# Attention's phases in the order outputs, corrections, scores, transposes, in place of scores, corrections, outputs, transposes

## The reference

```python
# q: 16 heads of 64; k, v: 2 heads of 64; blocks of 128 tokens; window of 128
kb = concat([previous block of k, this block], axis=2)     # vb the same
s = einsum('bnqkgd,bnskd->bnkgqs', q, kb) * HEAD_DIM ** -0.5
band = (sj <= qi + BLOCK) & (sj > qi + BLOCK - WINDOW)     # 128 keys per query
s = where(mask, s, -inf)
probs = softmax(concat([s, sink]))[..., :-1]
o = einsum('bnkgqs,bnskd->bnqkgd', probs, vb)
yb = (o * silu(a_gate)) @ w_br_attn
```

## Time and profile before

| | us |
|---|---|
| median of three runs | 1083.79 |
| the profiled execution | 1083.33 |
| its span | 1081.4 |
| PE busy | 1076.3 |
| DVE busy | 859.7 |
| ACT busy | 494.5 |
| POOL busy | 378.3 |
| scores of round 4 to scores of round 15 | 549.56 to 648.60 |

### The profile page before, as it was taken

How to read it: one execution, slowest core, us unless ns; L and a number is a source line. 1 busy time by engine, 2 the same in 40 slices (tenths; PEclk the granted TensorE clock), 3 DMA queues, 4 the chain that set the end, 5 groups by cost and what they waited for, 6 DMA issues and landing times.

```text
span 1081.4 us, 16517 instructions
## 1 busy us (share of the span) xinstructions
PE 1076.3 (100%) x6056; PEld 878.4 (81%) x6056; DVE 859.7 (79%) x1233; ACT 494.5 (46%) x961; POOL 378.3 (35%) x303
## 2 busy tenths in 40 slices
PE   9999999999999999999999999999999999999998
PEld 8888888888888888888777777888888888888887
DVE  5998998989999895775899987567669767376775
ACT  6643353443334444632666665424437335344332
POOL 1059888887878879753000101000000000000000
PEclk9999999999999999999999999999999999999999
DMA  9902231421334233748778686555545743334655
GB/s 347 364 1 79 78 118 43 154 80 40 127 112 142 78 138 97 246 155 249 211 220 206 208 207 223 194 172 178 176 135 195 255 156 117 97 118 139 209 177 195
DMA packets 65595, 173.85 MB, mean 161 GB/s; under 512 B 6776, under 2 KB 15736, under 8 KB 63192
## 3 DMA queue, kind: packets, MB, share of 16 engines
q1 hardware_dynamic: 39376, 100.64, 27.9%
q10 hardware_dynamic: 22688, 51.26, 14.4%
q0 software_dynamic: 3456, 20.97, 7.3%
HBM read 133.29 MB, written 55.41 MB: 174 GB/s over the span
## 4 chain that ended last, share of the span: by engine, by line
PE 96%; DVE 2%; DMA 0%; ACTq 0%; ACT 0%; issue 0%; POOL 0%; DVEq 0%; POOLq 0%
PE psg L981 38%; PE psg L787 22%; PE psb L1229 13%; PE psg L1139 8%; PE psg L818 2%; PE psb L1046 2%; PE psg L1110 2%; PE psg L901 1%; PE psg L1229 1%; PE psg L1170 1%; PE psb L1170 1%; PE psg L847 1%; PE psg L1182 1%; PE psg L1064 1%; PE psb L901 1%; PE psg L1105 1%
## 5 line engine op out<-in xcount | busy, mean ns | idle before, releaser
L1287 POOL TENSOR_TENSOR pair_w<-early_raw,pair_w 128x512 fp32r<-128x512 f32 x143 | 193.3, 1362 | 90.1 <-ACT pair_w L1495 90.1
L981 PE MATMUL psg<-early_hi,pair_w 128*128 128x512 f32 x704 | 216.9, 389 | 0.1
L981 PE MATMUL psg<-h_hi,pair_w 128*128 128x512 f32 x528 | 162.6, 389 | 0.0
L981 PEld LDWEIGHTS psg<-early_hi,pair_w 128*128 128x128 f32 x704 | 132.1, 188 | 27.9 <-POOL pair_w L1287 0.5
L1495 ACT ACTIVATE pair_w<-early_raw 128x512 fp32r<-128x512 f32 x143 | 87.1, 626 | 135.5 <-POOL early_raw L1303 94.4
L2175 DVE SCALAR_TENSOR_TENSOR psb<-conv,cols,psb 128x510 f32<-128x510 f32 (+6 forms) x196 | 137.3, 741 | 0.0
L981 PE MATMUL psg<-early_lo,pair_w 128*128 128x512 f32 x352 | 136.9, 389 | 0.0
L981 PEld LDWEIGHTS psg<-h_hi,pair_w 128*128 128x128 f32 x528 | 99.1, 188 | 20.6
L1270 POOL TENSOR_TENSOR rstd<-mean_sq,expo 128x4 f32<-128x4 f32 x3 | 3.1, 1021 | 298.0 <-DVE mean_sq L1978 279.1
L981 PE MATMUL psg<-h_lo,pair_w 128*128 128x512 f32 x264 | 102.7, 389 | 0.0
L1964 DVE TENSOR_TENSOR w_lo<-w_raw,w_hi 128x1024 fp32r<-128x1024 f32 x49 | 60.0, 1225 | 40.5 <-ACT w_hi L1408 37.2
(11 more groups left out here) (352 smaller groups left out, 2375.3 us busy)
## 6 DMA issues: line engine op xcount, KB each, us to landing
w_raw<-weights SPq DMA_DIRECT2D x52, 512.0 KB, 3.5
gates<-ring ACTq DMA_DIRECT2D x30, 512.0 KB, 3.2
w_sums<-w_pairs POOLq DMA_DIRECT2D x12, 1024.0 KB, 9.0
ring<-gates ACTq DMA_DIRECT2D x24, 512.0 KB, 4.3
early_raw<-w_pairs SPq DMA_DIRECT2D x11, 1024.0 KB, 5.5
early_raw<-w_pairs SPq DMA_DIRECT2D x11, 768.0 KB, 4.4
block_raw<-w_sums SPq DMA_DIRECT2D x32, 256.0 KB, 3.1
block_raw<-w_pairs SPq DMA_DIRECT2D x24, 256.0 KB, 3.5
```

The costliest lines, as they stand in the source:

```text
L981: mm = nc.tensor.matmul(bank, pair_w[:, at_w, w, k * P:(k + 1) * P], r[:, k, :], start=(not onto and k == 0 and m == 0), stop=(k == KP - 1 ...
L1287: nc.gpsimd.tensor_tensor(pair_w[:, at_w, 1, :], early_source(s, n), pair_w[:, at_w, 0, :].bitcast(F32), ALU.subtract).then_inc(early_spli ...
```

## The change

In each round from p = 3 on, `outputs(p - 2)` is called ahead of the two `scores` calls. Inside `outputs`, the outputs proper come first and open the accumulation (`start=True`), and the corrections follow and close it; each keeps the wait that stood ahead of it, and the last correction (in block 0 the last output) signals `pv_done`. The waits `half_evicted` and `o_ready` stay at the head of `outputs`.

```diff
@@ def outputs(p):
                 if p > 0:
                     pe.wait_ge(o_ready, p)
+                pe.wait_ge(pt_copied, 2 * p + 2)
+                for side in range(2):
+                    for par in range(2):
+                        mm = nc.tensor.matmul(out_of(p, side, par), vmix[:, n, gs], heads_of(pt_all[:, side], par),
+                                              start=True, stop=(n == 0))
                 if n > 0:
                     pe.wait_ge(pt_masked, 2 * p - 2)
                     pe.wait_ge(vstep_ready, 2 if n <= 2 else 4 if n <= NB // 2 else 7)
@@
-                                nc.tensor.matmul(out_part(p, side, par, part), vstep[rows, n - 1, dims],
-                                                 heads_of(pt_prev[rows], par), start=True, stop=False)
-                pe.wait_ge(pt_copied, 2 * p + 2)
-                for side in range(2):
-                    for par in range(2):
-                        mm = nc.tensor.matmul(out_of(p, side, par), vmix[:, n, gs], heads_of(pt_all[:, side], par),
-                                              start=(n == 0), stop=True)
+                                mm = nc.tensor.matmul(out_part(p, side, par, part), vstep[rows, n - 1, dims],
+                                                      heads_of(pt_prev[rows], par), start=False, stop=True)
                 mm.then_inc(pv_done, 1)
@@ def attention(p):
+                if p > 2:
+                    outputs(p - 2)
                 scores(p, 0)
                 scores(p, 1)
                 if p > 2:
-                    outputs(p - 2)
                     turn(p - 1)
```

## The result

The changed kernel takes 1094.46 us (median of five runs, 1094.27 to 1095.71), the kernel before, beside it, 1083.68. The ratio is 1.0098 with a 95% interval of 1.0087 to 1.0109: 10.8 us slower. The prediction was 1092.3 us, in a range of 1089 to 1097. The profiled execution has a span of 1092.5 us, 11.1 more than before.

The account below looks back on a forecast made before the run. PE was taken to bound the kernel, busy 1076.3 of 1081.4 us. 9.75 - 1.2 = +8.55 us on the profiled 1083.33 gives 1091.9; with 0.46 for the median, 1092.3 us, range 1089 to 1097 for 8 in 10.

Parts of the forecast that it names:

- The wait that loses its cover: At the head of `outputs`, PE waits for ACT's gate eviction without scores between: 0.75 us in 13 rounds, 9.75 us.
- PE's loads pulled ahead of the wait: At the outputs' first weight load: loading ahead of the wait would take off 1.8 us; not counted in the forecast.
- The order of shapes: On PE, corrections ahead of scores gain 0.10 us in 12 rounds: -1.2 us, between -2.0 and +1.7.
- The tail at the change: Leaving PE's 64x32 shape: shorter after a score (0.27 to 0.30 us) than after a correction (0.376 us).
- the count of changes: PE's shape changes per round, four before and four after: by count alone no gain, and a sum of 9.75 us.
- Scores that come later: DVE and ACT work behind the later scores stays covered, by 0.2 us at tightest; their loop takes 9.2 of 9.65 us.
- The slower loop: Rival: hand-overs through DVE and ACT make the attention round 10.1 us, 5.9 us more, 1098.2 us; chance 0.10.
- Nothing is given back: Behind attention no lost time returns; the rival had 3.4 us returning, 1088.9 us, chance 0.05 for +1 to +5.
- The clock: Rival: PE's stop in every round lowers its clock to 1.2 GHz, 74 us more, 1166 us; chance 0.01.

Follow-up runs that it names:

- twice_new: The changed kernel, with ACT evicting each round's gates twice, first into a scratch buffer; 1101.88 us, ratio 1.0183 to the kernel before.
- half_new: The changed kernel, with ACT evicting only 256 of the 512 columns of each round's gates; 1092.53 us, ratio 1.0088 to the kernel before.
- twice_old: The kernel before, in its old order, with ACT evicting each round's gates twice; 1086.03 us, ratio 1.0019.
- scores_between: The changed kernel with scores and corrections exchanged: outputs, scores, corrections, transposes; 1093.94 us, ratio 1.0095 to the kernel before.
- covered: The changed kernel, with outputs, corrections, scores and transposes started behind the round's first six gate matmuls instead of ahead of them; 1097.95 us, ratio 1.0109 to the kernel before.
- covered_low: As `covered`, with DVE splitting the next gate weights ahead of a round's maxima instead of behind the masks; 1090.57 us, ratio 1.0065 to the kernel before.

## Why the prediction was right

- *The wait that loses its cover*, 0.75 us a round, 9.75 in all: right in place and size. At the boundary shown it is 1.07 - 0.32 = 0.75, and the release takes the 0.05. `twice_new` and `half_new` show that the eviction's length goes into the round nearly one for one (0.20 us less for 0.22, 0.50 more for 0.48), `twice_old` that it is hidden in the old order until 1.1 us. One reading in the working is off without harm: in the old order the wait stood 1.11 us after the scores' start (604.62 against 603.51), at the corrections, and not 1.68. The cover to spare was 0.41 us, 0.36 with the release.
- *PE's loads pulled ahead of the wait*: the rule (the Trainium skill, "TensorE: Matmul & The Clock Gate", on the engine's queue), if it reached past a semaphore wait, would have taken 1.8 us off. In each of the 13 waits the load side waits too, and longer, 14.6 us against PE's 9.2, and in the boundary shown the first load starts with its matmul, at 600.48. Nothing came off.
- *The order of shapes*, -1.2 us: this term was wrong, the runs show 0. The step that failed was the start of the scores behind the corrections, put at 0.26 to 0.34 us and measured at 0.45. So the round is 9.77 and not 9.65. The tail at the change is indeed shorter (1.23 for the scores as against 1.25 taken), but the hand-over inside the shape takes back what it gives: 1.68 in both orders, as `scores_between` shows. The Trainium skill, "TensorEngine Tiling (Array Packing)", Key Properties, has a change of mode drain the engine; the count of changes, the other reading in the prediction, was the better one here: four changes before and after make no difference, and a fifth one costs 0.16 to 0.17 us. This term is over half of the difference between forecast and result.
- *Scores that come later*: right that they cost nothing in the rounds. DVE now waits for them (13.7 us). In the round after 8, which I had put at 0.2 us of spare time, `normalise` ended at 602.86 and the transposes began at 603.18; the list gives that idle time on the load side to DVE, but it is as short as in the other rounds (0.25). Not seen: round 3, where ACT is late (0.23), and the weight split behind the last round (0.4), which I had put at no cost. With the shape term's 1.2 and the 0.4 of scatter these make up the 2.2 us between forecast and result.
- *The slower loop*: not reached, at 9.77; `covered` shows rounds of 9.27 and the chain of `covered_low` the loop itself at 9.25, against the 9.2 worked out, or 9.3 with the corrections' 0.45.
- *Nothing is given back*: right, 409.5 us behind attention against 409.4.
- *The clock*: right. With a stop of 0.69 us in every round it stayed at 1.00 in the whole window of attention. The one fall in these traces, in `covered`, came behind a single stop of 2.73 us.

## What to carry to other kernels

A wait that costs nothing has a price that only its cover hides: before moving an instruction, list what it waits for and how long the moved-away work ran beside that, here 1.11 us of scores over a 0.60 us eviction and its release. Giving the wait a new cover isn't enough if the cover is itself moved past its own inputs (the gate weights' split), or if the work that it delays closes a loop over other engines; add up that loop against the round before and after. For tiled matmuls count the changes of shape: here two blocks of equal shape side by side could be exchanged at no cost, and a block of another shape between them cost 0.16 us a round.

## What was not expected of the hardware

- Between two blocks of the same 64x32 shape the next block's first matmul comes 0.45 us after the start of 16 corrections of 256 columns, and 1.11 us after the start of 64 scores of 160 columns; the sum with the other block is 1.68 us either way.
- One more change of shape in a round costs 0.16 us, measured twice (9.16 against 9.00, 9.94 against 9.77), though PE's load side is idle for 0.25 to 0.41 us at each change.
- Thirteen stops of 0.7 to 0.9 us, one in each round, left the granted clock at 1.00; one stop of 2.73 us was followed by 0.50.
- An eviction of 256 columns instead of 512 saves ACT 0.22 us of 0.60.
